# Attention inside a hybrid block: four buffers for the probabilities and row statistics in place of two, and the value product of a group one query tile later in the queues

## The reference, cut to what matters

```
F = cumsum(log_sigmoid(f))                      # per head
for i in range(8):                              # blocks of 128 queries
    s = q[lo:hi] @ k[:hi].T * 64**-0.5          # causal prefix of keys
    s = where(mask, s + F[lo:hi, None] - F[None, :hi], -inf)
    p = softmax(s)
    out_block = p @ v[:hi]
```

## Time and profile before

| | |
|---|---|
| median of 3 runs | 1558.69 us (1557.92 to 1559.14) |
| time of the profiled execution | 1557.71 us |
| its span, first to last instruction | 1556.0 us |
| TensorE busy in the span | 1434.0 us, 92% |
| mean granted TensorE clock | 0.976 |
| attention, from its third set of scores to its last value product | 112 to 446.5 us |

### The profile page before, as it was taken

One profiled execution on the slowest core, in us unless ns is written; L12 is line 12 of the kernel. 1 busy time (PEld: TensorE's weight loads), 2 busy tenths in 40 slices (PEclk: granted clock), 3 DMA queues, 4 the chain that ended last, 5 costly groups with the idle time before them and its releaser, 6 DMA issues.

```text
span 1556.0 us, 17915 instructions
## 1 busy us (share of the span) xinstructions
PE 1434.0 (92%) x6576; PEld 1178.7 (76%) x6576; DVE 411.7 (26%) x647; ACT 431.0 (28%) x706; POOL 485.5 (31%) x285
## 2 busy tenths in 40 slices
PE   4988788787887999999999999999999999999997
PEld 4976666666665788888878888888888888888885
DVE  4533443434356211111353211111111111113213
ACT  4443443434342211112342111111111112223322
POOL 1133343424333222223442221212212123444443
PEclk9998999999998999999999999999999999999999
DMA  5211021111132212233451111111111121243522
GB/s 177 44 30 22 21 43 28 35 31 35 34 95 68 41 55 40 46 49 122 162 188 43 54 41 54 48 46 54 40 54 40 54 67 68 92 144 118 173 94 95
DMA packets 113337, 106.77 MB, mean 69 GB/s; under 512 B 6576, under 2 KB 89008, under 8 KB 113264
## 3 DMA queue, kind: packets, MB, share of 16 engines
q1 hardware_dynamic: 111568, 99.94, 22.7%
q10 hardware_dynamic: 1728, 6.29, 1.2%
HBM read 93.89 MB, written 12.32 MB: 68 GB/s over the span
## 4 chain that ended last, share of the span: by engine, by line
PE 67%; DVE 3%; ACT 1%; issue 1%; DMA 0%; SPq 0%; POOL 0%; POOLq 0%; DVEq 0%
PE ps L1434 45%; PE ps L1694 21%; DVE pool_lo L1246 0%; DVE win L1262 0%; DVE head_tmp L1270 0%; PE ps L1743 0%; DMA pscale<-in_pool_scale 0%; DVE y_out L1062 0%; DVE y L1312 0%; DVE pool L1271 0%; PE ps L1573 0%; DVE h_lo L1318 0%; DVE win L1261 0%; DMA at_d<-at_st 0%; DVE pt_lo L1182 0%
## 5 line engine op out<-in xcount | busy, mean ns | idle before, releaser
L501 POOL TENSOR_TENSOR w_lo<-w_raw,w_hi 128x1024 fp32r<-128x1024 f32 (+1 forms) x141 | 338.4, 2401 | 761.0 <-ACT w_hi L669 760.8
L1434 PE MATMUL ps<-h_hi,w_hi 128*128 128x512 f32 x1152 | 298.6, 402 | 22.7 <-ACT u_st L739 6.9
L1434 PE MATMUL ps<-h_lo,w_hi 128*128 128x512 f32 x1152 | 290.3, 392 | 0.0
L1434 PE MATMUL ps<-h_hi,w_lo 128*128 128x512 f32 x1152 | 286.9, 390 | 0.0
L1434 PEld LDWEIGHTS ps<-h_hi,w_hi 128*128 128x128 f32 x1152 | 219.7, 193 | 71.8 <-ACT u_st L739 7.7
L1434 PEld LDWEIGHTS ps<-h_lo,w_hi 128*128 128x128 f32 x1152 | 215.7, 189 | 44.4
L1434 PEld LDWEIGHTS ps<-h_hi,w_lo 128*128 128x128 f32 x1152 | 215.5, 188 | 44.5
L669 ACT ACTIVATE w_hi<-w_raw 128x1024 fp32r<-128x1024 f32 (+1 forms) x141 | 145.5, 1035 | 279.7 <-PE ps L1434 278.6
L570 POOL TENSOR_TENSOR p_raw<-p_raw,rowinv 128x128 f32<-128x128 f32 (+3 forms) x64 | 73.2, 1147 | 180.6 <-DVE rowinv L1172 179.9
L1694 PE MATMUL ps<-w_lo,lg_hi 128*128 128x512 f32 x344 | 108.5, 396 | 0.0
L1694 PE MATMUL ps<-w_hi,lg_lo 128*128 128x512 f32 x344 | 108.5, 396 | 0.0
(11 more groups left out here) (168 smaller groups left out, 1500.4 us busy)
## 6 DMA issues: line engine op xcount, KB each, us to landing
w_raw<-in_w_ffn_down SPq DMA_DIRECT2D x88, 256.0 KB, 2.7
w_raw<-in_w_in SPq DMA_DIRECT2D x50, 256.0 KB, 5.8
w_raw<-in_w_ffn_gate SPq DMA_DIRECT2D x44, 256.0 KB, 3.1
w_raw<-in_w_ffn_up SPq DMA_DIRECT2D x44, 256.0 KB, 3.2
w_raw<-in_w_out SPq DMA_DIRECT2D x32, 256.0 KB, 2.8
xt<-in_x SPq DMA_DIRECT2D x8, 512.0 KB, 3.3
x<-in_x SPq DMA_DIRECT2D x8, 512.0 KB, 4.6
x_d<-x SPq DMA_DIRECT2D x8, 512.0 KB, 5.7
```

Source lines behind the costliest of these rows:

```text
L501: g.tensor_tensor(lo[:, 0:width], w_raw[c % 2][:, 0:width], hi[:, 0:width].bitcast(f32), ALU.subtract).then_inc(s_wlo, 1)
L1434: ins = mm(bank, stats[i], movs[i], start=first and i == 0, stop=last and i == n - 1)
```

## The change

`NPR` = 4 buffers take the place of 2 for `p_raw`, `negmax`, `rowsum` and `rowinv`. As tile `s` and tile `s+4` have their buffer in common, each is only as wide as the wider of the two needs: 640, 768, 896 and 1024 columns. The exponential of tile `s+2` now waits for the transposes of tile `s-2`. `values` of a group moves from the end of TensorE's step `s` (3, 7, 11, 15) into step `s+1`, between the fill and the transposes; that of group 3 moves into step 0 of the next pair, which has no fill. `evac_pv` moves from steps 4, 8, 12 and the end of the pair to the steps 5, 9, 13 and step 1 of the next pair, `v_high` and `v_low` of the odd head from step 1 to 2, and the store of group 3 behind the first weight loads of the next pair. `pv_tmp` is gone: ACT copies one half of the value product straight into `at_st`, which for odd groups now lies on partitions 64 to 127, and DVE adds the other half in place. `mask_f`, `tri` and `ones` move to a part of SBUF that attention uses again.

```diff
+NPR = 4
-        p_raw = [place(f"p_raw{i}", [P, S]) for i in range(2)]
+        p_raw = [place(f"p_raw{i}", [P, HALF + P * (i + 1)]) for i in range(NPR)]
-        pv_tmp = place("pv_tmp", [DH, HALF])
...
+                if p:
+                    store_at(p - 1, 3)
                 wait(sp, s_s, 16 * p)
                 load_frows(p, 1)
                 store_at(p, 0)
...
                 if p == 3:
                     load_branches(C_GATE + 4, 0, 0)
-                store_at(p, 3)
+                    store_at(p, 3)
...
-                g.tensor_tensor(p_raw[s % 2][:, 0:n], p_raw[s % 2][:, 0:n],
-                                rowinv[s % 2][:].to_broadcast([P, n]), ALU.mult).then_inc(s_pn, 1)
+                g.tensor_tensor(p_raw[s % NPR][:, 0:n], p_raw[s % NPR][:, 0:n],
+                                rowinv[s % NPR][:].to_broadcast([P, n]), ALU.mult).then_inc(s_pn, 1)
-                    if s == 1:
+                    if s == 2:
                         v_low(p, 1)
...
                 wait(act, s_mx, 16 * p + s + 1)
-                wait(act, s_th, RPAIR * p + RSUM[s - 1] if s > 0 else RPAIR * p - ROUNDS[15])
-                wait(act, s_rc, 16 * p + s - 1)
+                wait(act, s_th, RPAIR * p + RSUM[s + 1 - NPR] if s + 1 >= NPR
+                     else RPAIR * (p - 1) + RSUM[s + 17 - NPR])
+                wait(act, s_rc, 16 * p + s + 1 - NPR)
...
             def evac_pv(p, g4):
                 wait(act, s_pv, 4 * p + g4 + 1)
-                wait(act, s_pvev, 4 * p + g4)
-                a.activation(pv_tmp[:], ps[DH:2 * DH, 6, :], ACT.Copy).then_inc(s_pvt, 1)
+                wait(act, s_atst[g4 % 2], 16 * (2 * p + g4 // 2))
+                other = slice(DH * (1 - g4 % 2), DH * (1 - g4 % 2) + DH)
+                a.activation(at_st[g4 % 2], ps[other, 6, :], ACT.Copy).then_inc(s_pvt, 1)
...
                     evac_t(p, s)
-                    if s in (4, 8, 12):
+                    if s in (5, 9, 13):
                         evac_pv(p, s // 4 - 1)
-                    if s == 1:
+                    if s == 1 and not first:
+                        evac_pv(p - 1, 3)
+                    if s == 2:
                         v_high(p, 1)
...
-                evac_pv(p, 3)
...
                 wait(dve, s_pvt, 4 * p + g4 + 1)
-                wait(dve, s_atst[g4 % 2], 16 * (2 * p + g4 // 2))
-                v.tensor_tensor(at_st[g4 % 2][:], ps[0:DH, 6, :], pv_tmp[:], ALU.add).then_inc(s_pvev, 1)
+                own = slice(DH * (g4 % 2), DH * (g4 % 2) + DH)
+                v.tensor_tensor(at_st[g4 % 2], ps[own, 6, :], at_st[g4 % 2], ALU.add).then_inc(s_pvev, 1)
...
                     if s in (FILL_LAST if last else FILL):
                         fill(p, s, last)
+                    if s % 4 == 0 and s:
+                        values(p, s - 1)
+                    elif s == 0 and not first:
+                        values(p - 1, 15)
                     transposes(p, s, 0)
                     if s + AHEAD < 16 or not last:
                         scores(p, s + AHEAD)
                     if ROUNDS[s] == 2:
                         transposes(p, s, 1)
-                    if s % 4 == 3:
-                        values(p, s)
...
+            values(3, 15)
```

More of the change, by code:

```diff
@@ L135, in hybrid_block @@
         ident_r = place("ident_r", [P, P], f32r)
-        mask_f = place("mask_f", [P, P])
         mask_r = place("mask_r", [P, P], f32r)
-        tri = place("tri", [P, P])
-        ones = place("ones", [P, P])
         neg_half = place("neg_half", [P, 1])
@@ L143, in hybrid_block @@
         rstd = place("rstd", [P, 24])
-        negmax = [place(f"negmax{i}", [P, 1]) for i in range(2)]
-        rowsum = [place(f"rowsum{i}", [P, 1]) for i in range(2)]
-        rowinv = [place(f"rowinv{i}", [P, 1]) for i in range(2)]
+        negmax = [place(f"negmax{i}", [P, 1]) for i in range(NPR)]
+        rowsum = [place(f"rowsum{i}", [P, 1]) for i in range(NPR)]
+        rowinv = [place(f"rowinv{i}", [P, 1]) for i in range(NPR)]
         pscale = place("pscale", [P, NG])
@@ L168, in hybrid_block @@
         fbias = place("fbias", [P, NH])
+        mask_f = place("mask_f", [P, P])
+        tri = place("tri", [P, P])
+        ones = place("ones", [P, P])
         at[0] = after_v
         vs = [place(f"vs{i}", [P, NT, 2 * DH], f32r) for i in range(2)]
-        at_st = [place(f"at_st{i}", [DH, HALF]) for i in range(2)]
+        at_both = place("at_both", [P, HALF])
+        at_st = [at_both[DH * i:DH * i + DH, :] for i in range(2)]
         q1 = [place(f"q1_{i}", [P, S], f32r) for i in range(2)]
@@ L371, in store_at @@
                 sp.dma_start(at_d[2 * p + g4 // 2, :, HALF * (g4 % 2):HALF * (g4 % 2) + HALF],
-                             at_st[g4 % 2][:]).then_inc(s_atst[g4 % 2], 16)
+                             at_st[g4 % 2]).then_inc(s_atst[g4 % 2], 16)
             wait(sp, s_z, 4)
@@ L757, in softmax_exp @@
                 wait(act, s_mx, 16 * p + s + 1)
-                wait(act, s_th, RPAIR * p + RSUM[s - 1] if s > 0 else RPAIR * p - ROUNDS[15])
-                wait(act, s_rc, 16 * p + s - 1)
+                wait(act, s_th, RPAIR * p + RSUM[s + 1 - NPR] if s + 1 >= NPR
+                     else RPAIR * (p - 1) + RSUM[s + 17 - NPR])
+                wait(act, s_rc, 16 * p + s + 1 - NPR)
                 b = 1024 * (s % 2)
-                a.activation(p_raw[s % 2][:, 0:n], ps_flat[:, b:b + n], ACT.Exp, bias=negmax[s % 2][:],
-                             accum_out=rowsum[s % 2][:]).then_inc(s_exp, 1)
+                a.activation(p_raw[s % NPR][:, 0:n], ps_flat[:, b:b + n], ACT.Exp, bias=negmax[s % NPR][:],
+                             accum_out=rowsum[s % NPR][:]).then_inc(s_exp, 1)
             def evac_t(p, s):
@@ L804, in _, with attention @@
             act.wait_ge(s_fst, 64)
-            def attention(p, last):
+            def attention(p, last, first=False):
                 for s in range(16):
@@ L840, in attention @@
                         v_high(p + 1, 0)
-                evac_pv(p, 3)
-            attention(0, False)
+            attention(0, False, True)
             with act.Fori(1, 3) as p:
@@ L846, in _ @@
             attention(3, True)
+            evac_pv(3, 3)
             act.wait_ge(s_pjev, fill_units(3, 10, True))
@@ L1166, in row_max @@
                 b = 1024 * (s % 2)
-                v.reduce_max(negmax[s % 2][:], ps_flat[:, b:b + n], axis=AX.X, negate=True).then_inc(s_mx, 1)
+                v.reduce_max(negmax[s % NPR][:], ps_flat[:, b:b + n], axis=AX.X, negate=True).then_inc(s_mx, 1)
             def row_inv(p, s):
                 wait(dve, s_exp, 16 * p + s + 1)
-                wait(dve, s_pn, 16 * p + s - 1)
-                v.reciprocal(rowinv[s % 2][:], rowsum[s % 2][:]).then_inc(s_rc, 1)
+                wait(dve, s_pn, 16 * p + s + 1 - NPR)
+                v.reciprocal(rowinv[s % NPR][:], rowsum[s % NPR][:]).then_inc(s_rc, 1)
             def evac_t(p, s):
@@ L1558, in transposes @@
                     ins = nc.tensor.transpose(ps[:, bank, P * k:P * k + P],
-                                              p_raw[s % 2][:, (4 * r + k) * P:(4 * r + k + 1) * P], ident[:])
+                                              p_raw[s % NPR][:, (4 * r + k) * P:(4 * r + k + 1) * P], ident[:])
                 ins.then_inc(s_th, 1)
```

## The result

The changed kernel takes 1479.41 us, median of four runs (1478.4 to 1480.06), against 1558.91 for the kernel before: a ratio of 0.948, 95% interval 0.947 to 0.950. The forecast of 1490 was 11 us too slow, and 1479.41 lies at the lower edge of the range, 1479 to 1527. The profiled execution took 1478.4 us, 79.3 less than the one before.

A forecast was written before the change was run, and what follows sets the result against it. TensorE bounds the kernel, but in attention latencies between engines do. Waits of 57.3 us and 15.6 of clock go, less 4 for missed waits: 68.9 off the profiled 1557.7 gives 1488.8, median 1490 us; range 1479 to 1527.

The forecast's parts named there:

- the fills' 19.5 us: Attention: TensorE's fills wait some 19.5 us for ACT to copy the last fill out of bank 7.
- The walk's tightest place, step 5: Fill following step 5 of a middle pair: its wait of 1.93 us becomes about 0.1.
- The twelve waits inside pairs: Waits of values in steps 3, 7 and 11 of four pairs, 25.9 us, vanish because a fill covers each.
- the moved queue entries: SP's store of group 3 ahead of load_frows, and v_low a step later: priced at nothing, 12 us of cover.
- C: Rival: the store holds SP's queue, rows of F come late, scores of tile 8 stop TensorE; 1580 us; chance 0.04.
- D: Rival: nothing happens, each wait in attention returns elsewhere on its chain; 1558.7 us; chance 0.04.
- B: Rival: row maximum holds the exponential, only cover by fills works; gain 26 to 37 us, 1522 to 1533; chance 0.18.
- the sum: Whole kernel: 57.3 us of waits and 15.6 of clock go, less 4 for missed waits: gain 68.9 us.
- The walk: A middle attention pair stepped through with traced durations; from it 8.9 of 66.2 us of TensorE's waits stay.
- the 4 us: Allowance of 1 us for each attention pair for missed small waits, also meant to hold VectorE and GpSimd contention.
- one stretch of half clock: Attention: one stretch like that from 214 us on stays, some 3.4 us long, 1.7 lost.
- Rival A: Attention: the waits go but the half clock stays; gain 53.3 us, 1505 us; chance 0.13.

The follow-up runs named there:

- Experiment 1: Changed kernel with four buffers, but values, evac_pv, v_high, v_low and the store in their old places; 1498.97 us, ratio 0.961.
- Experiment 2: Kernel before with its two buffers, but values and evac_pv in their later place; 1523.15 us, ratio 0.977.
- experiment 3: Changed kernel with values ahead of the fill in steps 4, 8 and 12, so without a fill's cover; 1496.55 us, ratio 0.960.
- Experiment 6: Changed kernel with GpSimd's second w_low (chunk 7) moved to step 1 of the next pair, behind the scaling of tile 3; 1473.25 us, ratio 0.945.
- the first kernel of experiment 5: Kernel before, two buffers, with evac_t(s) ahead of exp(s+2) and the fill's copy in ACT's list, ahead of row_inv(s+2) in DVE's; 1531.2 us, ratio 0.983.

## Why the prediction was right or wrong

**Right: the mechanism of the buffers.** The exponential behind the transposes made ACT late, and the fills' 19.5 us came from there. Experiment 1 removes them with the buffers alone. Experiment 2 keeps them with the late `values` alone. The walk's tightest place, step 5, was to wait 0.1 us; it does not appear in the list.

**Right: cover and its absence.** `values` was to wait once a pair, 1.6 us in three pairs and 1.8 in the last, about 7 us; it waits 6.6. The twelve waits inside pairs were to vanish; they did, and experiment 3 shows that it takes the fills to do it: without them 16 stops stay.

**Right: the moved queue entries cost nothing.** No scores wait for a load. Rivals C and D fell with the time; B fell with the fills' waits, which are gone in the changed kernel and in experiment 1: the exponential does wait for the row maximum, 70 us in all, but almost all of it under the cover of a fill.

**The step that failed is the sum, above all a term that it lacks: what a stop of TensorE costs beyond its listed wait.** It had nothing for this, and 6.8 us came from there. I go through its terms.

*The waits.* The walk left 8.9 us, and I took off 4 more: *"The walk surely misses small waits; I take off 1 us for each pair, 4"*. Together 12.9 us were to stay, and 12.2 stayed, so the size was right within 0.7. The kind was not: the walk missed no small waits all over the pair, but one wait, three times, that of the transposes of tile 2 for GpSimd, 1.7 us where I had 0.2. I had put the neighbourhood of VectorE and GpSimd aside in the 4 us, with 2.91 against 2.39 us as the only price. The copy of `k` was priced at nothing and takes 2.78 us in place of 0.69, and the two `w_low` take 1.0 us more. Experiment 6 gives these waits back. That the allowance fits in size is luck.

*The clock.* I kept, besides the entrance, one stretch of half clock that loses 1.7 us; none stayed in the pairs 1 to 3. The 0.95 of pair 0 over 65.8 us is 6.6 us at the half level, 3.3 lost, so 17.0 of the 20.3 us came back and not 15.6. Rival A is out.

*The missing term.* 54.0 us of waits and 17.0 of clock are 71.0, and attention is 77.4 us shorter. TensorE's busy time fell from 268.5 to 244.7 us, 23.8, of which the clock explains 17.0. The other 6.8 us go with 34 stops less, 0.20 us for each. The matmul in front of a wait is listed with its whole latency, about 0.4 us, where the next one in a stream starts after 0.23; so a stop may cost a part of that beyond its listed wait. Two kernels compared by themselves scatter: 3.0 us by the medians and 4.4 by the traces for the 12 stops of experiment 3; and the first kernel of experiment 5, with 39 stops, was busy 255.7 us up to its last `values`, 248.6 without the half clock (7.1 lost), against 241.4 for the changed kernel with 9 stops, 7.2 us for 30. Over all twelve traces, from 5 stops (241.0 us busy without the half clock) to 43 (248.4), a straight line gives 0.20 us for each stop, and no trace lies more than 1.0 us off it. The size is measured; that the drain is what costs it is argued, not shown.

*After attention.* I had it unchanged; it is 1.9 us shorter. Counted from the end of the last `values`, the ten traces of the experiments have 1107.5 to 1109.4 us there, the changed kernel 1107.6 and the kernel before 1109.5; what sets this stays open.

So the miss of the gain, 79.3 measured against 68.9 in the profiled executions, is 10.4 us: 6.8 from the stops, 1.9 behind attention, 1.4 of clock and 0.7 of waits, less 0.4 by which these terms overshoot attention (54.0 + 17.0 + 6.8 = 77.8 against 77.4). By the same price the 24 stops of experiment 1 in place of 43 should be near 4 of the 9 us by which it beat its expectation; its own trace shows some 2.

## What to carry to other kernels

Where an in-order engine has work for tile `s+2` ahead of work for tile `s`, and both wait for the same event because of a buffer, it is the buffer that makes one of them late; more buffers free both, a swap only chooses the late one. Walk such a schedule through with the durations of the trace: here the walk met the waits of `values` and of the fills within 0.1 us. It does not see two things. One is the price of a stop beyond its listed wait, here about 0.2 us. The other is what a change that brings work forward makes run side by side: the forwarded copy met a GpSimd instruction and gave part of the gain back.

## What the runs showed of the hardware

A VectorE copy of 64 x 1024 float32 to fp32r takes 0.69 us when GpSimd does nothing beside it. Begun while GpSimd is in a `tensor_tensor` on SBUF with 0.45 us or more to go, it takes 1.00 to 2.79 us. This is no fixed factor: all 27 slow copies in attention, in five kernels and six traces, end 0.54 to 0.56 us behind the end of that GpSimd instruction, whether 0.5 or 2.2 us of it were left. So the price is what is left of GpSimd's instruction, as if the copy stood still until then. The two instructions in front of it in pair 1 fit the same rule: the `tensor_tensor` of `q`, begun at 176.69 beside the first `w_low`, ends 1.08 us behind it, and the second `w_low` ends 2.26 us behind that `tensor_tensor` and takes 3.39 us. Each of the three ends behind the one it met by 0.14 us less than the time that it takes alone (0.69, 1.22 and 2.40). That they stand still until then is inferred from these ends. The Trainium skill ("GPSIMD Engine Reference", 1. Specifications) names VectorE's 2-port modes and instructions with two SBUF inputs as those that contend with GpSimd. The trace agrees for the `tensor_tensor` of `q`, which has two SBUF inputs and takes 1.51 us beside a `w_low` where the kernel before has 1.22; whether the copy, which has one input, runs in such a mode no run here shows. A row maximum of 768 columns, read out of PSUM, takes 0.95 us beside the second `w_low` of experiment 6, as all eight of that kernel do on average. The slow copy vanished in experiment 6, which moves GpSimd's instruction alone.

TensorE ran at the full clock through all of pairs 1 to 3 with 6 stops of 1.6 to 1.8 us; with 24 stops in all (experiment 1) it did too, behind the entrance, until the last wait of the last pair, 1.83 us, behind which eight matmuls took 2.42 and eight more 2.67 us where the changed kernel has 1.75 and 1.73 behind a wait of the same length. So the length of a single wait does not decide whether the clock falls; I have not found what does.
